# Two-block model on one core: weight rounding placed ahead of the pieces behind each product, running sums behind the mask

## The reference, cut to what matters

```
f = lb + (1 - lb) * sigmoid(f_pre); k = 1 - f; log_f = log(f); qa = silu(q)
bcum = cumsum(log_f inside a chunk)
q_dec = qa * exp(bcum); k_inv = k * exp(-bcum)
scores = where(causal, q_dec @ k_inv^T, 0); o_intra = scores @ v
o_inter = q_dec @ state; state = exp(blast) * state + k_end^T @ v
o = rms_norm(o) * norm_w * silu(g)
```

## Time and profile before

| | us |
|---|---|
| median of 3 timed runs | 2882.61 |
| the three runs | 2882.61, 1887.61, 2883.52 |
| the profiled execution | 1880.63 |
| its span (first to last instruction) | 1878.8 |
| TensorE busy (matmuls) | 1795.9 (96%) |
| VectorE busy | 1164.6 (62%) |
| ScalarE busy | 740.0 (39%) |
| mean granted TensorE clock (of 1) | 0.979 |

### The profile page before, as it was taken

How to read it: one execution, slowest core, us unless ns; L and a number is a source line. 1 busy time by engine, 2 the same in 40 slices (tenths; PEclk the granted TensorE clock), 3 DMA queues, 4 the chain that set the end, 5 groups by cost and what they waited for, 6 DMA issues and landing times.

```text
span 1878.8 us, 27193 instructions
## 1 busy us (share of the span) xinstructions
PE 1795.9 (96%) x11004; PEld 1555.2 (83%) x11004; DVE 1164.6 (62%) x1798; ACT 740.0 (39%) x1097; POOL 8.2 (0%) x10
## 2 busy tenths in 40 slices
PE   8999999999999999999988888989999899999997
PEld 5777877778788888888988778879988899999885
DVE  5666656656577777434745455666788777777423
ACT  5344333332443333334443445343354533333221
POOL 0000000000000000000000000000000000000000
PEclk9999999999999999999999989989999999999999
DMA  5222222223233232332211111112212232232331
GB/s 189 79 79 79 90 88 70 73 90 97 90 90 99 93 101 90 101 92 87 80 46 57 46 57 55 59 56 70 79 58 68 64 95 91 91 91 90 101 99 59
DMA packets 44332, 154.23 MB, mean 82 GB/s; under 512 B 5792, under 2 KB 6048, under 8 KB 44208
## 3 DMA queue, kind: packets, MB, share of 16 engines
q1 hardware_dynamic: 44208, 152.50, 25.8%
HBM read 150.39 MB, written 2.10 MB: 81 GB/s over the span
## 4 chain that ended last, share of the span: by engine, by line
PE 74%; DVE 13%; ACT 7%; issue 2%; DVEq 2%; ACTq 1%; DMA 0%; SPq 0%
PE ps L590 73%; ACT arena L893 4%; DVE arena L1242 4%; DVEq L1733 2%; DVE arena L1249 2%; DVE w_lo L1239 2%; ACTq L1222 1%; ACT L898 1%; ACT L893 1%; PE ps L594 1%; ACT w_hi L893 1%; DVE arena L1245 1%; DVE arena L1256 1%; DVE h_res L1239 1%; DVE arena L1578 0%
## 5 line engine op out<-in xcount | busy, mean ns | idle before, releaser
L590 PE MATMUL ps<-u_hi,w_hi 128*128 128x264 f32 (+3 forms) x2376 | 654.2, 329 | 13.1 <-DVE w_lo L1239 9.1
L590 PE MATMUL ps<-u_hi,w_lo 128*128 128x264 f32 (+3 forms) x2376 | 645.4, 325 | 0.0
L590 PE MATMUL ps<-u_lo,w_hi 128*128 128x264 f32 (+3 forms) x2376 | 643.2, 324 | 0.0
L1239 DVE TENSOR_TENSOR w_lo<-w_raw,w_hi 128x1024 fp32r<-128x1024 f32 x280 | 342.4, 1223 | 212.7 <-ACT w_hi L893 204.2
L590 PEld LDWEIGHTS ps<-u_hi,w_hi 128*128 128x128 f32 (+1 forms) x2376 | 400.2, 191 | 59.7 <-DVE w_lo L1239 9.7
L590 PEld LDWEIGHTS ps<-u_hi,w_lo 128*128 128x128 f32 (+1 forms) x2376 | 399.5, 190 | 37.1 <-issue 2.0
L590 PEld LDWEIGHTS ps<-u_lo,w_hi 128*128 128x128 f32 (+1 forms) x2376 | 398.6, 190 | 36.4 <-issue 1.1
L893 ACT ACTIVATE w_hi<-w_raw 128x1024 fp32r<-128x1024 f32 x280 | 297.0, 1061 | 207.2 <-PE ps L590 176.0
L1249 DVE SCALAR_TENSOR_TENSOR ffn<-full,par,ffn 128x512 f32<-128x512 f32 (+2 forms) x176 | 132.2, 751 | 81.0 <-ACT ffn L893 77.8
L893 ACT ACTIVATE arena<-arena 128x528 f32<-128x528 f32 (+8 forms) x189 | 96.5, 533 | 194.4 <-DVE arena L1242 71.0
L893 ACT ACTIVATE ffn<-full,par 128x512 f32<-128x512 f32 x88 | 67.8, 771 | 267.1 <-DVE full L1242 267.1
(11 more groups left out here) (140 smaller groups left out, 1526.3 us busy)
## 6 DMA issues: line engine op xcount, KB each, us to landing
w_raw<-weights SPq DMA_DIRECT2D x280, 512.0 KB, 3.5
h_res<-xT SPq DMA_DIRECT2D x4, 512.0 KB, 6.8
outT<-h_res SPq DMA_DIRECT2D x8, 256.0 KB, 2.1
cst<-consts SPq DMA_DIRECT2D x1, 730.0 KB, 10.4
seg<-consts SPq DMA_DIRECT2D x1, 256.0 KB, 10.4
par<-params SPq DMA_DIRECT2D x1, 244.0 KB, 2.6
msk<-cmask SPq DMA_DIRECT2D x1, 128.0 KB, 10.5
h_res<-metaT SPq DMA_DIRECT2D x1, 64.0 KB, 10.0
```

The source lines that it names most:

```text
L590: return nc.tensor.matmul(out, lhsT, rhs, start=start, stop=stop)
L1239: return V.tensor_tensor(out, a, b, op)
```

## The change

Three edits.

1. On ScalarE, a group is followed at once by the rounding of the next slab (`group_and_slab`), ahead of the pieces behind the group. Before, that slab was rounded behind the pieces, at the start of the next group or inside `prep`. For groups of 8 units it is the same slab, and each slab is still rounded once.
2. On VectorE, `prep` of an HGRN2 head no longer splits a slab ahead of its own operations; that slab's w_lo is made at the start of the next group, behind them.
3. On VectorE, the running sum of head n (`prep_ln`, now `prep_sum`) stands behind the masked copy of `head_a(n-1)`, no longer ahead of it. On ScalarE `prep_ln` stays where it was.

```
@@ schedule
         put("hi", h, ("prep_exp", n))
         if h:
             put("hq", h, ("head_a", n - 1))
+        put("hq", h, ("prep_sum", n))
+        if h:
             put("hi", h, ("head_b", n - 1))
             put("hg", h, ("head_c", n - 1))
         put("hg", h, ("prep", n))
@@ scalar
+            def group_and_slab(g):
+                group(g)
+                split_until(min(SLABS, FIRST_UNIT[g + 1] // PER + SPL))
+
-            stages = {... "group": group, ...}
+            stages = {... "group": group_and_slab, ...}
@@ vector
                 i = n - GLA_H
-                low_weights(GROUP_OF[("hg", i)] + 1)
                 dve.wait_ge(exp_ok, n + 1)
...
-            def prep_ln(n):
+            def prep_sum(n):
                 dve.wait_ge(sp_ok, n + 1)
                 link(V.tensor_tensor_scan(bc2, seg16, lf2, 0.0, ALU.mult, ALU.add))
...
-            stages = {... "prep_ln": prep_ln, ...}
+            stages = {... "prep_sum": prep_sum, ...}
```

More of the change, by code:

```diff
@@ L1214, in ssm_sum @@
                 f(r, r, ACT.Exp, scale=-0.5).then_inc(S["r"], 1)
-            stages = {"raw": raw, "raw_meta": raw_meta, "slab": lambda s: split_until(s + 1), "square": square, "norm": norm, "bounds": bounds, "group": group, "prep": prep, "prep_ln": prep_ln, "prep_exp": prep_exp, "head_a": head_a, "head_b": head_b, "head_c": head_c,
+            stages = {"raw": raw, "raw_meta": raw_meta, "slab": lambda s: split_until(s + 1), "square": square, "norm": norm, "bounds": bounds, "group": group_and_slab, "prep": prep, "prep_ln": prep_ln, "prep_exp": prep_exp, "head_a": head_a, "head_b": head_b, "head_c": head_c,
                       "head_d": head_d, "swa_v": swa_v, "swa_a": swa_a, "swa_b": swa_b, "ssm_dt": ssm_dt,
@@ L1724, in ssm_v2 @@
                                        op0=ALU.mult, op1=ALU.subtract).then_inc(tile_lo, 1)
-            stages = {"raw": raw, "raw_meta": raw_meta, "slab": lambda s: low_until(s + 1), "square": square, "norm": norm, "bounds": bounds, "second_start": second_start, "group": group, "prep": prep, "prep_ln": prep_ln, "head_a": head_a, "head_b": head_b,
+            stages = {"raw": raw, "raw_meta": raw_meta, "slab": lambda s: low_until(s + 1), "square": square, "norm": norm, "bounds": bounds, "second_start": second_start, "group": group, "prep": prep, "prep_sum": prep_sum, "head_a": head_a, "head_b": head_b,
                       "head_d": head_d, "swa_a": swa_a, "swa_c": swa_c, "ssm_dt": ssm_dt,
```

## The result

| | us |
|---|---|
| before, comparable runs | 1887.61, 1887.89 (the profiled execution: 1880.63) |
| after, four runs | 1840.92, 1841.55, 1843.21, 1844.46; median 1842.38 |
| ratio of comparable runs | 0.976, 95% interval 0.9737 to 0.9784 |
| span of the profiled execution | 1839.8 (before 1878.8) |

By these runs the change makes the kernel 2.4% faster; the forecast was 1844. How much faster is less sure than the interval looks. The ratio has two runs of before behind it, and both lie at the upper end of what this kernel took in the 30 runs of before taken with the experiments, 1865.22 to 1889.34 us. The two traces differ by 39.0 us, which is 2.1% of 1878.8. Four executions stay out of every ratio, and no trace shows their cause: two of before near 2883 us, one of E3 at 2882.87 (mean granted clock 0.557) and one of E1 at 3487.79 (1.00 on record).

The account below looks back on a forecast made before the run. TensorE, busy 96%, bounds the kernel; gains come only from its waits and low clock. 1880.6 us less 43.5 (35.8 + 3 + 4.7) plus 7 for the clock gives 1844; own range 1834 to 1863, extended to 2886 for slow runs.

Parts of the forecast that it names:

- six heads at full clock: Six HGRN2 head periods, each 6.0 us shorter with TensorE at full clock: 35.8 us gained.
- the clock in the heads: Granted clock falling behind the seven waits left in the HGRN2 heads: 7 us given back, bounds 0 and 21.7.
- the first head: First HGRN2 head: its wait ahead of `head_b` falls from 2.59 to some 0.4 us, less low clock: 3 us.
- behind the last head, Mamba part: Behind the last HGRN2 head a wait and low clock go, less new waits: 4.7 us; Mamba part taken as 0.
- the first block: Rounding moved ahead of a chain in the first block's 4 heads: loss between 0 and 4.2 us, taken as 0.
- The walk through a head: One HGRN2 head step by step: no wait ahead of `head_a`, 2.0 us ahead of `head_b`, period 33.9 us.
- the 34 named as a sign: Lower end of the 34 to 37 us head period that would show the forecast right.
- half of them at 2 us: Clock price: half of seven waits of about 2 us have a fall costing 2 us each, 7 us back.
- Rivals 1 and 2: Clock stays up in all heads, 1837 us, chance 0.18; or falls in every head, 1859 us, chance 0.14.
- new waits between 50 and 250 us: Sign of a wrong forecast: new waits in that stretch of the run.
- Rival 3: ScalarE's chain 3 us longer per head, so `head_b` waits 5 us: 1862 us, chance 0.08.
- Rival 4: Roundings not hidden, each moved ahead of a piece TensorE waits for costs 1.06 us: 1907 us, chance 0.05.

Follow-up runs that it names:

- E3: Only the running sum moved behind the masked copy on VectorE, against the kernel before; 1861.68 us, ratio 0.992.
- E1: Only ScalarE's rounding of the next slab moved ahead of the pieces, against the kernel before; 1891.09 us, ratio 1.0079.
- E2: Only VectorE's slab ahead of `prep` taken out, against the kernel before; 1836.62 us, ratio 0.9805.
- E9: E4 with ScalarE's early rounding added only behind the last HGRN2 head; 1823.72 us, ratio 0.969.
- E4: The change with ScalarE's early rounding undone, both VectorE edits kept; 1824.86 us, ratio 0.9737.
- E8: E4 with VectorE's slab for the product hi made one group later; 1828.2 us, ratio 0.9719.
- E5: The change with ScalarE's early rounding in the second block only; 1838.41 us, ratio 0.9774.
- E7: The change without ScalarE's early rounding in the first block and behind hq and mb; 1827.83 us, ratio 0.9722.

## Why the total came near, and which steps of the prediction failed

Forecast 1844, with a range of its own from 1834 to 1863, measured 1842.38; and the mechanism is the one that the prediction walked through. What it had wrong is how much the change saves. It took a change within two per cent for the likeliest (0.54), its own sum being 36.6 us of 1880.6, 1.95%. Measured were 45.4 us against the comparable runs of before, 2.4%, and 39.0 between the traces. Its terms, beside what the table of stretches has for them:

| term of the sum | predicted | measured |
|---|---|---|
| six heads at full clock | 35.8 | 38.6 |
| the clock in the heads | -7 | -4.6 |
| the first head | 3 | 4.2 |
| behind the last head, Mamba part | 4.7 | 6.0 |
| the first block | 0 | -5.1 |
| sum | 36.5 | 39.1 |

**The steps that failed** are three. The first block, put at 0 with no row behind it, lost 5.1 us. The six heads, 35.8 less 7 for the clock, were taken 5.2 too small: they gave 34.0. These two errors have opposite signs, so that the total came within 2.6 us is luck. And the sum starts at 1880.6, the profiled execution, while the comparable runs of before took 1887.61 and 1887.89, 7.1 more, where the median of after lies only 0.8 above its own profiled execution. This makes 6.3 of the 8.8 us between 36.6 and 45.4. Taken from 1887.75, two per cent would have been the line 1850 and not 1843, and the forecast of 1844 would have lain beyond it. One by one:

- **The walk through a head** was right to 0.4 us at each step (the table of steps). Edit 2 was the cause that it named, and E2 shows it alone. A period at full clock became 33.5 (from 1035.65 to 1069.12), predicted 33.9; the six periods took 33.4 to 35.1 us, three of them less than the 34 named as a sign. The difference of 0.4 arises in two places. The copies started 0.26 early: the evacuation of hq came 0.11 early, and from there it was 5.75 us and not 5.9, since the rounding overlaps the tanh ahead of it. And the small copies were to start 1.09 behind the large ones and hold `head_b` for 0.47 more; four copies went through in 1.38, and `head_b` started 0.05 later. So the wait is 1.46, not 2.0. For six heads at full clock that is 239.45 - 6 x 33.48 = 38.6 gained, for 35.8.
- **The clock.** The step "half of them at 2 us", for seven waits, was sized at 7. It measured 4.6: three of the six heads had a fall, of 1.5 us each (9.02 us from 965.62 to 974.64, against 7.50), and the seventh wait, 1.29 us at 1170.83, had none. Half of seven was near, and the price of 2 was too high. Rivals 1 and 2, no fall and one in every head, both missed. The waits that were left are shorter than those they were priced from, but that this is why isn't shown: the last section has longer waits without a fall.
- **The first head** brought 4.2, for 3; **behind the last head and in the Mamba part** it was 6.0, for 4.7 and about 0. E2 and E9 divide it: 2.5 come with edit 2 alone, 3.3 with edit 1 (E9 against E4). In the change as made one wait in the Mamba part went up by 1.05 (3.45 us ahead of the ac_st product at 1347.03, before 2.40 at 1385.07), as predicted, and the wait of 1.90 for `h_res` behind it went.
- **The first block** rests on this sentence: "a chain that TensorE doesn't wait for now; no row here tells how near it is to being late", taken at 0 with 4.2 as the bound. It measured 5.1, of which 3.4 are shown to be edit 1's. The prediction had named "new waits between 50 and 250 us" as a sign of being wrong, and they are there, at 101.25, 149.17 and 197.33. A row of before did tell: w_lo ends at 98.77 and the product that reads it starts at 98.87, with no wait recorded. I had looked for ScalarE's pieces as the thing that is late, not for the slab that VectorE makes behind its wait for them. The start of the run, with 1.25 of the 5.1 us, I had not looked at.
- **Rival 3** fell with the walk: the chain wasn't longer. Behind the table load at 1032.20 (1.28 us) the Ln starts at 1033.50. The Trainium skill, "ScalarE: Activation LUTs", What ACT_TABLE_LOAD costs, has 2.66 us for a switch with its drain; these rows have room for no more than the load itself, since the rounding ahead of it ends at 1032.14 and the Ln follows 0.02 us behind its end.
- **Rival 4** (the roundings aren't hidden, 1907) was wrong as a whole and right in kind: E1, without edit 2, is 0.8% slower. In the change as made edit 1 costs 3.4 to 4.5 us in the first block and 13.8 in the heads (E4's against its own), and gives 3.3 to 3.8 behind them. The prediction had edit 1 in its walk twice ("one rounding, 1.06 and a gap, ahead of it: 13.95"; "plus 1.08 ... 24.8"), and its own numbers would have given E4: without the two, `head_b` could start at 24.2, and TensorE is there at 24.45. It asked what the change as a whole does and never which part of it pays.

## What to carry to other kernels

Where an in-order engine prepares operands ahead of their use, each such piece belongs behind the work that somebody waits for and no earlier than its own user needs: price it in each chain that it stands in, since one placement rule cost 3.4 to 4.5 us in the first block and 13.8 in the heads, and gained 3 to 4 behind them. A later place isn't free either: in E8 the slab only moved into another chain. A wait of zero in the profile isn't slack: before adding work to a chain, subtract the end of what it makes from the start of the instruction that reads it. Count a gain from the same kind of run with which it will be compared: 7 us between two executions of one kernel were a fifth of this gain. And undo the parts of a change one by one, since the two best kernels here, E9 and E4, which can't be told apart by their times, do without most or all of the edit for which the change was named.

## What was not expected of the hardware

- Short waits of TensorE, 1.46 us in each of six heads that ran the same instructions, were followed by a fall of the granted clock in three heads and not in the other three; in E5, with the same waits, in two; behind 1.36 to 1.39 (E2) in one; behind 1.7 us (E3) in each of six (`head_b` to `head_c` 8.99 to 9.01 us), behind 0.5 (E7) in none. The length of the wait doesn't decide it alone. In the same heads of E3 TensorE waits 2.26 to 2.28 us ahead of `head_a`, and no fall follows that; it comes only behind the shorter wait 11 us later (one head: `head_a` at 953.26, `head_b` at 964.27; granted clock 1.00, then 0.81):

```profile
953.00:964.00 11.00, 9.31 (x92) 7.61 (x92) 7.34 (x11) 6.19 (x10) 0.00 (x0) 1.00 0.17 49
964.00:973.00 9.00, 8.73 (x58) 8.61 (x59) 5.05 (x10) 4.21 (x8) 0.00 (x0) 0.81 0.39 110
```

  Two stretches of 2 us in the kernel after, behind waits of 1.46 and 1.47, the first with a fall:

```profile
968.00:970.00 2.00, 2.00 (x11) 2.00 (x11) 1.71 (x6) 0.78 (x3) 0.00 (x0) 0.50 0.72 203
...
1038.00:1040.00 2.00, 2.00 (x19) 2.00 (x18) 1.71 (x6) 0.81 (x3) 0.00 (x0) 1.00 0.81 190
```

  The engine had done the same work ahead of both (busy 28.54 of the 30 us from 938, 28.53 of the 30 from 1008). A wait of 1.5 us so costs 1.5, or 3.0. The Trainium skill, "TensorE: Matmul & The Clock Gate", What's actually happening, lets the place of a change of clock differ from run to run; here it differs between equal heads of one run.
- Four copies of `head_a` on ScalarE, two large and two small, take 1.38 us together; two large alone took 1.09 and two small 0.42.
- A rounding starts 0.56 us behind the start of a tanh of 128x528 (1030.54, 1031.10) that is itself listed with 0.65; in E4 one starts 0.78 behind the start of an Exp of that size (1011.33, 1012.11).
